# Seven products for a gate and the next queries in two branches of a hybrid decoder layer

## What is computed

```python
def hybrid_layer(x, pos, key_valid, rel_bias, top_k, w_in, b_f, g_q, g_kv, w_uq, w_ukv, sinks, w_out, ln_g, ln_b):
    B, P, _ = x.shape
    h = split_cols(x @ w_in)
...
    out_a = causal_dense_attention(qa, ka, va, key_valid, HEAD_DIM ** -0.5, decay)
    out_b = mla_attention(h['b_cq'], h['b_ckv'], h['b_kr'], g_q, g_kv, w_uq, w_ukv, pos, key_valid)
...
    mixed = jnp.concatenate([
        out_a * jax.nn.silu(h['a_g']), out_b * jax.nn.silu(h['b_g']),
        out_c * jax.nn.silu(h['c_g']), out_d * jax.nn.silu(h['d_g'])], axis=-1)
    y = mixed @ w_out
    return layer_norm(ALPHA * x + y, ln_g, ln_b)
```

## Time and profile before

| | |
|---|---|
| time, three runs | 2845.45, 2845.72 and 2848.62 us |
| median | 2845.72 us |
| profiled execution: span | 2845.6 us |
| TensorE busy | 2800.3 us, 98% |
| VectorE busy | 1727.4 us, 61% |
| ScalarE busy | 1073.7 us, 38% |
| GpSimd busy | 644.7 us, 23% |
| instructions | 39703 |

### The profile page before, as it was taken

How to read it: one execution, slowest core, us unless ns; L and a number is a source line. 1 busy time by engine, 2 the same in 40 slices (tenths; PEclk the granted TensorE clock), 3 DMA queues, 4 the chain that set the end, 5 groups by cost and what they waited for, 6 DMA issues and landing times. The chain is left out here.

```text
span 2845.6 us, 39703 instructions
## 1 busy us (share of the span) xinstructions
PE 2800.3 (98%) x13562; PEld 1650.8 (58%) x13562; DVE 1727.4 (61%) x4511; ACT 1073.7 (38%) x3094; POOL 644.7 (23%) x1353
## 2 busy tenths in 40 slices
PE   8999999999999999999999999999999999999998
PEld 6446666655566666644464466666555666666443
DVE  4337988767787423355433379887677864333565
ACT  4234444334455444510032344443335554455000
POOL 1002333112133244510000023331111322355000
PEclk9999999999999999999999999999999999999999
DMA  6101110111111012052320011111111100211521
GB/s 239 46 24 47 45 43 31 42 34 32 51 26 33 23 30 112 16 161 67 112 111 18 24 47 45 45 34 36 38 46 40 29 23 22 97 45 34 169 87 44
DMA packets 91998, 160.10 MB, mean 56 GB/s; under 512 B 11600, under 2 KB 67552, under 8 KB 90008
## 3 DMA queue, kind: packets, MB, share of 16 engines
q1 hardware_dynamic: 91800, 157.57, 16.9%
HBM read 123.34 MB, written 32.08 MB: 55 GB/s over the span
## 5 line engine op out<-in xcount | busy, mean ns | idle before, releaser
L1352 PE MATMUL ps_s<-xT,w_ring 128*128 128x348 f32 (+4 forms) x3616 | 1124.8, 462 | 8.0 <-ACT feat L1578 2.0
L1352 PEld LDWEIGHTS ps_s<-xT,w_ring 128*128 128x128 f32 x3616 | 665.7, 190 | 379.7 <-issue 93.4
L1631 ACT ACTIVATE arena<-ps_t 16x32 f32<-16x32 f32 (+3 forms) x1048 | 368.9, 375 | 304.9 <-PE ps_t L1423 289.6
L1618 ACT ACTIVATE arena<-arena,small 128x1040 f32<-128x1040 f32 (+8 forms) x544 | 372.0, 684 | 196.8 <-DVE small L1965 196.7
L1658 DVE MAX8 small<-score 128x8 f32<-128x1040 f32 (+6 forms) x448 | 376.0, 839 | 9.9
L1660 DVE MATCH_REPLACE8 score<-small,score 128x1040 f32<-128x1040 f32 (+6 forms) x448 | 369.8, 825 | 0.0
L2084 POOL TENSOR_SCALAR strips<-arena,small 128x16 f32<-128x16 f32 x384 | 108.0, 281 | 869.7 <-DVE small L1977 869.7
L1423 PE MATMUL ps_t<-ident,arena 128*128 128x128 f32 (+1 forms) x2016 | 299.3, 277 | 0.6 <-ACT cT L1552 0.6
L1396 PE MATMUL ps_s<-feat 64*128 64x272 f32 (+12 forms) x1680 | 294.7, 453 | 0.0
L2087 POOL TENSOR_SCALAR arena<-arena,small 128x1024 f32<-128x1024 f32 (+7 forms) x384 | 287.7, 749 | 0.0
L1423 PEld LDWEIGHTS ps_t<-ident,arena 128*128 128x128 f32 (+1 forms) x2016 | 225.6, 139 | 105.8 <-issue 59.1
(11 more groups left out here) (254 smaller groups left out, 2727.1 us busy)
## 6 DMA issues: line engine op xcount, KB each, us to landing
w_ring<-in_w_feat SPq DMA_DIRECT2D x78, 512.0 KB, 3.5
mixed<-mixg SPq DMA_DIRECT2D x128, 128.0 KB, 1.7
score<-resid SPq DMA_DIRECT2D x16, 512.0 KB, 5.5
feat<-mixed SPq DMA_DIRECT2D x16, 512.0 KB, 6.4
arena<-in_w_out SPq DMA_DIRECT2D x4, 1536.0 KB, 8.3
resid<-score SPq DMA_DIRECT2D x9, 512.0 KB, 3.0
cT<-falls SPq DMA_DIRECT2D x8, 520.0 KB, 4.8
feat<-falls SPq DMA_DIRECT2D x8, 520.0 KB, 5.4
```

The source lines that it names most:

```text
L1352: mm = pe.matmul(ps_s[:, bank, 0:w], w_ring[:, wt % 2, k, :], xT[:, k, c0:c0 + w], start=(k == 0), stop=(k == KT - 1))
L1618: nc.scalar.activation(p, p, ACT.Exp, scale=-1.0, bias=nm[:, e:e + 1], accum_out=psums[0:M, st % 4, e:e + 1]).then_inc(S["exp_done"], 1)
L1631: a = nc.scalar.activation(dst, src, ACT.Copy)
```

## The change

In A's four pairs and D's pairs 0 to 2 (`UNITS`, `joined`), seven in a layer, the pair's gate and the next pair's queries no longer come from two tiles of eight products each. They are taken together as one 2 x 2 problem: the rows are gate and queries, the inner dimension is cut in two halves of four 128-tiles, and the tokens in two halves of 520 (layer 1: 512). `unit` makes it from seven products P1 to P7 of half size, as in the scheme of Strassen and Winograd; eight would be the plain way. Each product is made for two quarters j = 1, 0 of the tokens, of 260 columns each (layer 1: 256), by four matmuls.

Four of the products multiply sums of weights: GpSimd makes S3, S1, S2 and S4 (`ws7`), 128 x 512 each, once a unit. Four multiply sums of x, T1, T3, T2 and T4: GpSimd makes them once a layer, 8,320 columns in all (`xs`), in the index stage, pair 1. P2 and P3 go on top of P1 and P5 in the same bank. ScalarE copies P1 out (these are the new queries' first part) and takes the tanh of P2's bank and later of the low gate (`gl`); VectorE does the rest out of PSUM into the query tile and `gate`. In A some products and all key chunks go to score banks (`next_bank`: the next step's; `this_bank`: the step's own), the others to `P_BANK`. In `TOP_RATE`, A has 32 searches a pair for 39, B 46 for 38. `A_SCALE` is applied to the keys and no more to the queries. B's weights `w_tb` are loaded in D pair 0, step 3 (`tb`), into another place, and the rotary tables, on which T1 lies meanwhile, in D pair 2, step 5 (`tab`).

```diff
+UNITS = "AD"
+PART_OF_X = {"P1": "B11", "P2": "B21", "P6": "T2", "P7": "T3", "P5": "T1", "P3": "B22", "P4": "T4"}
+PART_OF_W = {"P1": "A11", "P2": "A12", "P6": "S2", "P7": "S3", "P5": "S1", "P3": "S4", "P4": "A22"}
+W_SUMS = ["S3", "S1", "S2", "S4"]
+X_SUMS = [("T1", 0, 4), ("T3", 0, 4), ("T2", 0, 4), ("T4", 0, 2), ("T4", 2, 4)]
...
-TOP_RATE = {"A": [3, 4, 5, 5, 6, 4, 5, 5, 2], "D": [4, 4, 4, 4, 4, 4, 4, 4, 4], "D3": [4, 4, 4, 4, 4, 3, 2, 3, 3],
-            "B": [4, 4, 5, 5, 5, 5, 5, 4, 2], "C": [0] * 9}
+TOP_RATE = {"A": [2, 3, 4, 4, 4, 4, 4, 4, 3], "D": [4, 4, 4, 4, 4, 4, 4, 4, 4], "D3": [4, 4, 4, 4, 4, 3, 2, 3, 3],
+            "B": [5, 5, 5, 5, 6, 6, 5, 5, 4], "C": [0] * 9}
...
+def halves_of(l):
+
+    return (N_META, BLK * 2) if l == DEPTH - 1 else (0, NTOK // 4)
+
...
+    def unit(self, l, br, p):
+
+        to, at = (br, p + 1) if p + 1 < NP else ("D", 0)
+        wg = self.open("G", br, p)
+        wq = self.open("AQ" if to == "A" else "Q", to, at)
+        u = self.take("unit")
+        self.left[wg] = self.left[wq] = 4
+        base = dict(l=l, br=br, p=p, u=u, wg=wg, wq=wq, to=to, at=at)
+        nth = {}
+
+        def product(m, j, bank):
+            by = "act" if m == "P1" else "dve"
...
+            it = self.add("sp", m=m, j=j, done=done, gin=gin, after=dict(nth),
+                          **self.group(by, bank, scored=m in ("P4", "P5")), **base)
+            nth[m, j] = it["nth"]
...
-                for idx, work in zip((3, 4, 5), self.tile(l, "Q", br="D", p=p + 1)):
+                for idx, work in zip((3, 4, 5), self.tile(l, "Q", br="D", p=p + 1) if not joined else []):
                     put(idx, work)
+                if p == 0:
+                    put(3, lambda: self.add("tb", l=l))
...
-            late = 2 if br == "A" and idx < 3 else 0
+            late = 2 if br == "A" and (joined or idx < 3) else 0
...
+        if br == "A":
+            keys = self.tile(l, "AK", p=p + 1) if p + 1 < NP else self.tile(l, "K", br="D")
+        product, sums, low = self.unit(l, br, p)
+
+        def one(idx, m, j, bank):
+            put(idx, lambda: product(m, j, bank()))
+
...
+        if br == "A":
+            for idx, work in enumerate(keys):
+                put(idx, lambda work=work: work(bank=next_bank))
+            one(0, "P1", 1, p_bank)
+            one(1, "P2", 1, p_bank)
+            one(2, "P1", 0, p_bank)
+            by_side(3, sums)
+            one(3, "P2", 0, p_bank)
+            one(4, "P6", 1, next_bank)
+            one(4, "P7", 1, p_bank)
+            one(5, "P6", 0, next_bank)
+            one(5, "P5", 1, p_bank)
+            one(6, "P4", 1, next_bank)
+            one(6, "P3", 1, p_bank)
+            one(7, "P7", 0, next_bank)
+            by_side(7, lambda: low(1))
+            one(7, "P5", 0, p_bank)
+            put(8, last_of_all)
+            one(8, "P3", 0, p_bank)
+            self.carried.append(lambda: low(0))
+        elif br == "D":
+            one(0, "P1", 1, this_bank(0))
+            one(0, "P1", 0, p_bank)
+            one(0, "P2", 1, this_bank(0))
+            put(1, sums)
+            one(1, "P2", 0, p_bank)
+            one(2, "P6", 1, this_bank(0))
+            one(2, "P6", 0, this_bank(1))
+            one(3, "P7", 1, this_bank(0))
+            one(3, "P7", 0, this_bank(1))
+            one(3, "P5", 1, p_bank)
+            one(4, "P3", 1, p_bank)
+            one(4, "P5", 0, this_bank(0))
+            one(4, "P4", 1, this_bank(1))
+            one(4, "P3", 0, this_bank(0))
+            one(5, "P4", 0, this_bank(0))
+            put(5, lambda: low(1))
+            put(5, lambda: low(0))
+            if p == NP - 2:
+                put(5, lambda: self.tables(l))
...
+                elif kind == "tb":
+                    sp.wait_ge(S["pv_done"], 2 * it["upto"]["pv"])
+                    sp.dma_start(w_tb, t_in["w_tb"][l]).then_inc(S["vw_ld"], 16)
+                elif kind == "tab":
+                    sp.wait_ge(S["pj_full"], it["upto"]["pj"])
+                    sp.dma_start(cos_t, t_in["cos_t"]).then_inc(S["tab_ld"], 16)
+                    sp.dma_start(sin_t, t_in["sin_t"]).then_inc(S["tab_ld"], 16)
...
+                elif kind == "sp":
+                    m, j, u, bank, w = it["m"], it["j"], it["u"], it["bank"], halves_of(l)[1]
+                    for wt in (it["wg"],) if m in ("P1", "P2") else (it["wg"], it["wq"]):
+                        pe.wait_ge(w_ld[wt % 2], 16 * (wt // 2 + 1))
+                    if m in ("P5", "P6", "P7", "P3"):
+                        pe.wait_ge(S["w_sum"], len(W_SUMS) * u + W_SUMS.index(PART_OF_W[m]) + 1)
+                    if m in ("P5", "P6", "P7", "P4"):
+                        pe.wait_ge(S["x_sum"], X_PER_LAYER * l + (X_PER_LAYER if it["br"] == "C" else len(X_SUMS)))
...
+                    waits(pe, it["free"])
+                    w_of = part_of_w(it, PART_OF_W[m])
+                    for k in range(4):
+                        mm = pe.matmul(ps_s[:, bank, 0:w], w_of[:, k, :],
+                                       part_of_x(l, PART_OF_X[m], k, k + 1)[:, 0, w * j:w * j + w],
+                                       start=(k == 0 and m not in ("P2", "P3")), stop=(k == 3),
+                                       skip_group_check=m in ("P2", "P3"))
+                    mm.then_inc(S["pj_full"], 1)
...
-                        nc.scalar.activation(dst[:, cs], ps, ACT.Copy, scale=A_SCALE).then_inc(S["pj_act"], 1)
+                        nc.scalar.activation(dst[:, cs], ps, ACT.Copy).then_inc(S["pj_act"], 1)
                     elif what in ("AK", "K"):
                         dst = k_tile["A"][it["p"] % 2] if what == "AK" else k_tile[it["br"]][0]
-                        nc.scalar.activation(dst[:, cs], ps, ACT.Copy).then_inc(S["pj_act"], 1)
+                        nc.scalar.activation(dst[:, cs], ps, ACT.Copy, scale=A_SCALE).then_inc(S["pj_act"], 1)
...
+                elif kind == "sp" and it["m"] != "P1":
+                    m, j, after = it["m"], it["j"], it["after"]
+                    ps = ps_s[:, it["bank"], 0:halves_of(l)[1]]
+                    q = q_tile[it["to"]][it["at"] % 2]
+                    q_low, q_high = q[:, cols_of(l, "low", j)], q[:, cols_of(l, "high", j)]
+                    g_low, g_high = gate[:, cols_of(l, "low", j)], gate[:, cols_of(l, "high", j)]
+                    if m == "P2":
+                        dve.wait_ge(S["gate_in"], it["gin"] + 1)
+                        t = dve.scalar_tensor_tensor(g_high, g_high, 1.0, ps, ALU.add, ALU.mult)
+                    else:
+                        dve.wait_ge(S["pj_full"], it["g"] + 1)
+                        if m == "P6":
+                            dve.wait_ge(S["pj_act"], after["P1", j])
+                            t = dve.tensor_tensor(g_low, ps, q_low, ALU.add)
+                        elif m == "P7":
+                            dve.wait_ge(S["pj_dve"], after["P6", j])
+                            t = dve.tensor_tensor(q_high, ps, g_low, ALU.add)
+                        elif m == "P5":
+                            dve.wait_ge(S["pj_dve"], after["P7", j])
+                            t = dve.tensor_tensor(q_low, ps, q_high, ALU.add)
+                        elif m == "P3":
+                            dve.wait_ge(S["pj_dve"], after["P6", j])
+                            t = dve.tensor_tensor(g_low, ps, g_low, ALU.add)
+                        else:
+                            dve.wait_ge(S["pj_dve"], after["P7", j])
+                            t = dve.tensor_tensor(q_high, q_high, ps, ALU.subtract)
+                    t.then_inc(S["pj_dve"], 1)
...
+                elif kind == "ws7" and it["on"] == "pool":
+                    for wt in (it["wg"], it["wq"]):
+                        pool.wait_ge(w_ld[wt % 2], 16 * (wt // 2 + 1))
...
+                    for name, one, other, op in (("S3", "A11", "A21", ALU.subtract), ("S1", "A21", "A22", ALU.add),
+                                                 ("S2", "S1", "A11", ALU.subtract), ("S4", "A12", "S2", ALU.subtract)):
+                        n += 1
+                        nc.gpsimd.tensor_tensor(part_of_w(it, name), part_of_w(it, one), part_of_w(it, other), op
+                                                ).then_inc(S["w_sum"], 1)
+                        pool.wait_ge(S["w_sum"], n)
```

More of the change, by code:

```diff
@@ L648, in empty_step @@
+    def empty_step(self, l, br, p, early, work, aside):
         self.normalise()
@@ L2102, in feature_tiles @@
     tiles = []
[L2103 to L2107 removed]
+    for w, br, p in Plan().tiles[:MT_PER_LAYER]:
+        br = (br or "").lower()
+        tiles.append({"IK": lambda: ik, "IQ": lambda: r("c_iq", 128 * p, 128),
                           "AQ": lambda: r("a_q", 128 * p, 128), "AK": lambda: r("a_k", 128 * p, 128),
```

242 lines of the change are left out of this document (201 added, 41 removed).

## The result

The changed kernel takes **2884.9 us** (median of four runs, 2883.4 to 2887.6), the one before 2846.5 (2845.5 to 2848.6): a ratio of 1.0135, with 95% interval 1.0123 to 1.0147. I had forecast 2852, at most 2866. It is 38 us slower.

What follows compares the result with a forecast made beforehand. TensorE, busy 2800.3 of 2845.6 us, was taken to bound the kernel. Columns -48, old waits -4, new waits 2 x (13.8 + 13.9) and B +3 gave +6.4, so 2852 us; the 8-in-10 range was 2824 to 2866.

Steps and rivals of the forecast that it cites:

- 4 us of old waits: A and D: TensorE's old waits at the chunk products, 2.0 us a layer, go because other work stands there.
- -48 us: TensorE, A and D: seven units a layer save 28,896 columns, 48.7 us, less about 0.6 for 112 more matmuls.
- A: 13.8 a layer: A: new TensorE waits behind VectorE, 4.9 us in pairs 0 and 1, 2.4 in pair 2, 1.6 in pair 3.
- The mask wait: A step 4: VectorE stands still from 4.3 to 6.6 us because GpSimd's weight sums go before the mask.
- D: 13.9 a layer: D: products wait for scans of the banks they go to, 4.9 us in pairs 0 and 1, 4.1 in pair 2.
- GpSimd's sums ... cost D nothing: D: GpSimd's weight sums start at about 8.5 us, S2 is ready at 12.8, before P6, so they add 0.
- B: +3: B: the moved searches cost 0.4 us a pair, between bounds of 0 and 5.6, 3 us in all.
- The banks have two steps' slack: B: VectorE, busy 45.1 of 59.4 us in pair 0, can take the moved searches nearly free.
- eight more a pair: B: searches moved there by the new table, each about 0.7 us wide in pair 0.
- VectorE keeps up: Rival, A and D: copies fall into VectorE's idle time, half the waits remain, 2825 us, faster; chance 0.28.
- Slower still: Rival: a GpSimd-VectorE lock, or B unable to hold the searches, 4 to 14 us more, 2856 to 2866; chance 0.10.
- Break-even is 3.7 us: A and D: new waits in each of 14 units at which the change gains nothing; the forecast found 4.0.

Runs made afterwards that it cites:

- e8: Changed kernel with units in A alone, the mask ahead of A's weight sums and e5's table of searches: 2834.3 us, ratio 0.9959.
- e11: Kernel before the change with only e5's table of searches: 2855.8 us.
- e4: Changed kernel with A's four weight sums behind the mask of step 4 on GpSimd, not ahead of it: 2874.5 us.
- e3: Changed kernel with 62 of every 64 search passes left out in A and D, picked keys not the reference's: 2843.0 us.
- e15: e3 with D's weight sums cut to 8 columns of each 128, results not the reference's: 2827.8 us.
- e10: Changed kernel, units in A and D, with the mask ahead of A's weight sums and e5's table: 2849.2 us.
- e2: Changed kernel with units in A alone, D as before the change: 2862.9 us.
- e1: Kernel before the change with only the change's new table of searches, nothing joined: 2870.2 us, ratio 1.0086.
- e5: Changed kernel with another table of searches: A 30 a pair, two in step 8 for three, B's last pair 78: 2857.3 us.

## Why the prediction was wrong

The difference to the kernel before by stage, both layers, in us. Idle time and busy time of TensorE are from the traces; the busy time is split by the trace's record of the clock into work at full clock and what the lower level added. The forecast's 48 us of columns are divided by units:

| | A | D | B |
|---|---|---|---|
| new idle, forecast | 27.6 | 27.8 | 3 |
| new idle, measured | 28.2 | 34.1 | 6.7 |
| work, forecast | -27.4 | -20.6 | 0 |
| work, measured | -27.8 | -16.7 | 0.5 |
| lower clock, forecast | 0 | 0 | 0 |
| lower clock, measured | 4.9 | 11.4 | 0 |
| together, forecast | 0.2 | 7.2 | 3 |
| together, measured | 5.3 | 28.8 | 7.2 |

The forecast had 4 us of old waits gone besides, in A and D, which the measured idle time contains. So D holds about 22 of the 33 us beyond the forecast.

- **"-48 us" of columns: nearly right as work (44), short as time.** A column in A cost what it had cost; with waits in A and none of the lower clock, A's units give 21.5 of their 27.8 us (e8 against e11). In the changed kernel the lower clock added 16 us to TensorE's busy time, 11 of them in D. The sum had no such term, and the earlier trace rows could not show one: in its rows TensorE hardly waits. This is the first step that failed, and the largest. D's work fell by 4 us less than forecast; why stays open.
- **"A: 13.8 a layer": right.** 15.3 in layer 0, at the places named (scores of steps 5 and 6, the next pair's first scores, the key chunks, these about 1.0 each for 0.3); A pair 1 came out at 74.0, forecast 73 to 74. The mask wait was forecast as 2.3 and measured as 2.4; taking it away gave 10 us (e4), 1.3 a pair for the 1.2 in the sum.
- **"D: 13.9 a layer": the size right for the products in layer 0 (14.2), and so is the cause in pair 1, where VectorE behind four passes came last.** What failed is the other half, "GpSimd's sums ... cost D nothing": it held only as long as VectorE was later. The sums stood 0.65 us behind, and with the passes gone P6 still waited 1.8 to 2.4 us, for them (e3, e15). P1, P7 and P4 wait mostly 0.6 to 0.8 each for the scans of their own step's banks, whatever VectorE has to do. In pair 1 of e3 and of e10 the products' waits are 3.8 us, and a stretch at the lower clock behind P6's wait adds 1.7, against 3.4 forecast as saved. D's units lose in every pair of runs that differs by them: 22 us (after, e2) and 14.9 (e10, e8). D pair 1 came out at 71.3, forecast 66; of the difference 3.6 us are the clock (0.95 for 1.00) and 1.7 a wait in the latents' part (L1532 behind L2224), of which I had said nothing.
- **"B: +3": 7.2 measured,** 1.2 and 2.2 us in pairs 0 and 1 of layer 0, and all of it the table's, since e1 has the same 7.2. "The banks have two steps' slack" is not so for the gate: its product (L2138) wants the bank one chunk later, and 1.9 us of B's waits are that. The "eight more a pair" are seven.
- **The table had no price of its own.** The three passes of step 8 are in the sum, among A's 17 searches, so A came out right with them; the closing of a block, 1.0 us in two of A's pairs, is not. What I never asked is what the table does alone: 24 us without a single unit (e1), and 28 given back by another one (e5), 8 of them in D and 6 in B. It was the largest part of the loss, and no part of the products. This account and that of the clock overlap: with e5's table the lower clock adds 13.5 us for 21.1.
- **The rivals.** "VectorE keeps up" was wrong. "Slower still" named a lock and B: the lock gave nothing, B 4 of the 33 us beyond my forecast. The other side of the forecast, faster, is there for A alone (e8), with another table and order. "Break-even is 3.7 us" left B's 3 out; with it, it is (48 + 4 - 3) / 14 = 3.5.

## What to carry to other kernels

Where the bound engine gets shorter pieces of work, price each new wait and then what the engine's clock may do after it: here a wait of 2.4 us cost 4.1, and over the run such stretches cost 16 us more than before. When a table of filler work is changed beside the real change, run each alone, and read the shortest step first: here one pass more where a step lasts 2.8 us, with a block's closing beside it, outweighed seven fewer elsewhere. A product that goes to the bank of its own step's scores waits for their scan, whoever is idle, and removing one releaser shows little while another stands 0.5 us behind it.
